# Second block's attention: a loop over tiles rewritten as a pipeline of eight units

## The chip, the cores and the metric

One core of one Trainium2 chip. The metric is the device time of one execution in microseconds; each kernel is run several times and the median is shown. Times inside an execution come from one execution taken with the hardware profiler.

## The reference, cut to what matters

The program is a whole network of three layers on 512 tokens of width 1024, all in float32: a first block (a mixer of a gated delta rule and a sliding window attention, then a mixture of 32 experts), then a second block of two layers, one with windowed attention and one with a recurrent unit, each followed by an MLP. The change lies in the second block's attention alone:

```
qkv = h @ w_in                                   # 512 x 1024 times 1024 x 1536
q, k, v = split: 8 heads of q, 2 of k, 2 of v, 128 wide; q, k = partial_rope(q), partial_rope(k)
kb, vb = band(k), band(v)                        # blocks n-1, n, n+1 of 128 keys, zeros outside
scores = einsum("bnqhgd,bnjhd->bnhgqj", qb, kb) * 128 ** -0.5
valid  = (|qpos - kpos| <= 128) & (kpos >= 0) & (kpos < 512)
scores = where(valid, scores, -inf)
m = maximum(max(scores), sink);  p = exp(scores - m)
denom = sum(p) + exp(sink - m)
o = einsum("bnhgqj,bnjhd->bnqhgd", p / denom, vb);  return o @ w_out
```

Four tiles of 128 queries, each against three blocks of 128 keys. The block before tile 0 and the block after tile 3 don't exist and are masked out.

## The kernel before, in words

Each engine has its own instruction list; between them stand semaphores that the program sets and waits for by hand. An engine takes its list in order. `drain` waits until the engine's own earlier work is written. `meet` (at the end of each stage) is a barrier over TensorE (pe), VectorE (dve), ScalarE (act) and GpSimd (pool); SyncE, which issues the weight loads, waits for barriers with `reached`.

The stage around the change is `at_pe`, `at_dve`, `at_act` and `at_loads`. In front of it `comb_dve` (line 1866) gathers the experts' outputs into X tile by tile, and SyncE loads the three 512-column pieces of `attn_w_in` into slots 0 to 2 and those of `attn_w_out` into slots 4 and 5. `piece_pe` (957) turns a tile of X with eight transposes into two PSUM banks and `piece_act` (968) writes it, scaled and shifted, into `hT`. PSUM has eight banks of 512 columns, `ps[:, 0]` to `ps[:, 7]`.

Projections (lines 1987 to 1999): for each tile three products of eight matmuls (L1996) with 512 columns; ScalarE copies each to `qtok` (L2098) and frees the bank; four banks are used in turn. A float32 matmul shows as two records in the trace, a float32 transpose as one. On VectorE the rope is applied per tile (2045 to 2051), and one semaphore, `roped`, is set after the last tile.

Then, once: k of all tiles is turned by eight transposes (L2006), copied to `kTa` (L2055), which has zero blocks at both ends, and v is copied to `vpad` with zero blocks (L2058).

Then a hardware loop (`Fori`) over the four tiles, on all three engines:

1. VectorE copies q of the tile to `stage` (L2061), TensorE turns its eight heads (L2011), VectorE copies them to `qTb` (L2063).
2. For each head g of k: TensorE makes the scores of four heads of q against 384 keys (L2018, four matmuls into banks 0 to 3). VectorE scales them, adds the mask and writes them to SBUF (L2068), takes the maximum (L2070), joins the sink and negates (L2072 to L2075). The scores of g = 1 wait for `att_shifted` of g = 0, since they use the same banks.
3. ScalarE takes the exponentials with their sums (L2105, L2107).
4. For each g: TensorE turns the twelve blocks of probabilities (L2023, banks 4 to 6), ScalarE copies them out (L2111), TensorE multiplies with v (L2030, bank 7), VectorE divides by the sum and writes the output into `qtok` (L2085).
5. The next tile begins when both outputs are written.

After the barrier `o_pe` turns the outputs (L965) and multiplies with `attn_w_out` (L2127). SyncE begins to load the weights of the following MLP only after the same barrier.

The first block's sliding window attention (`sw_pe`, `sw_act`, `sw_dve`, lines 999 to 1093) is written as eight units of a tile and a head of k, with the scores made two units ahead: scores L1070, shift L1011, maximum L1013, exponentials L1046, transposes L1083, copy L1058, product with v L1092, output L1024. Its heads are 64 wide, and a unit has two blocks of keys (one in tile 0).

Of the kernel before, what the change touches and what calls it, by code (L numbers as in the profile page):

```python
# [6 lines left out]
ALU = mybir.AluOpType  # L7
ACT = mybir.ActivationFunctionType
AX_X = mybir.AxisListType.X
# [98 lines left out]
def build(nc, A, out, dbg=None):  # L108
# [8 lines left out]
    with ctx:  # L117
# [1862 lines left out]
        vpad = scratch[:, 4096:5632].rearrange("p (b n) -> p b n", b=6)  # L1980

        def at_loads(sp):
            sp.dma_start(rope, A["k_rope"].rearrange("p (t b n) -> p t b n", t=TT, b=2)).then_inc(S("at_in"), 16)
            sp.dma_start(gqb, A["k_gqbias"].rearrange("p (t n) -> p t n", t=TT)).then_inc(S("at_in"), 16)

        def at_pe(pe):
            piece_pe(pe, "3", 0, X[:, 0], 4)
            for t in range(TT):
                turned(pe, "3", t)
                for s in range(3):  # L1990
                    if t == 0:
                        take(pe, s)
                    i = 3 * t + s
                    pe.wait_ge(S("bank_free"), before("bank_free", "at") + i + 1)
                    for k in range(KT):
                        ins = pe.matmul(ps[:, i % 4], hT[:, k, t * P:(t + 1) * P], slots[:, s, k], start=k == 0, stop=k == KT - 1)  # L1996
                    ins.then_inc(S("product"), 1)
                    if s == 0 and t + 1 < TT:
                        piece_pe(pe, "3", t + 1, X[:, t + 1], 4)
            for s in range(3):  # L2000
                pe.drain().then_inc(freed[s], 1)

            pe.wait_ge(S("roped"), 1)
            for g in range(KH):
                for t in range(TT):
                    ins = pe.transpose(ps[:, 4 + g, t * P:(t + 1) * P], qtok[:, t, QH * HD + g * HD:QH * HD + (g + 1) * HD], ident[:])  # L2006
            ins.then_inc(S("k_turned"), 1)
            with pe.Fori(0, TT) as t:
                pe.wait_ge(S("att_normed"), t + 1)
                for h in range(QH):  # L2010
                    ins = pe.transpose(ps[:, 6 + h // 4, (h % 4) * P:(h % 4 + 1) * P], stage[:, h * HD:(h + 1) * HD], ident[:])  # L2011
                ins.then_inc(S("att_turned"), 1)
                pe.wait_ge(S("att_qk_ready"), t + 1)
                for g in range(KH):
                    if g:
                        pe.wait_ge(S("att_shifted"), t * 2 + (g + NU))
                    for j in range(QK):
                        ins = pe.matmul(ps[:, j, 0:3 * P], qTb[:, g * QK + j], kTa[:, g, bass.ds(t * P, 3 * P)], start=True, stop=True)  # L2018
                    ins.then_inc(S("att_scores"), 1)
                for g in range(KH):  # L2020
                    pe.wait_ge(S("att_exp"), t * 2 + (g + 1 + NU))
                    for j in range(12):
                        ins = pe.transpose(ps[:, 4 + j // 4, (j % 4) * P:(j % 4 + 1) * P], glogs[g][:, j // 3, (j % 3) * P:(j % 3 + 1) * P], ident[:])  # L2023
                    ins.then_inc(S("att_pturned"), 1)
                    pe.wait_ge(S("att_pT"), t * 2 + (g + 1 + NU))
                    if g:
                        pe.wait_ge(S("att_tile_done"), t * 2 + (g + NU))
                    for j in range(QK):
                        for b in range(3):
                            ins = pe.matmul(ps[:, 7, j * P:(j + 1) * P], gpT[:, 3 * j + b], vpad[:, bass.ds(t + b, 1), g * HD:(g + 1) * HD], start=b == 0, stop=b == 2)  # L2030
                    ins.then_inc(S("att_pv"), 1)
                pe.wait_ge(S("att_tile_done"), t * 2 + (2 + NU))

        def at_dve(v):
            v.memset(kTa, 0.0)
            v.wait_ge(S("at_in"), 32)
            v.drain()
            H = ROT // 2
            for t in range(TT):
# [17 lines left out]
            v.memset(vpad[:, 5], 0.0)  # L2057
            v.tensor_copy(vpad[:, 1:5], qtok[:, :, 1280:1536])  # L2058
            v.drain()
            with v.Fori(0, TT) as t:  # L2060
                v.tensor_copy(stage[:], qtok[:, t, 0:D]).then_inc(S("att_normed"), 1)  # L2061
                v.wait_ge(S("att_turned"), t + 1)
                v.tensor_copy(qTb.rearrange("p (b h) n -> p b (h n)", b=2), ps[:, 6:8]).then_inc(S("att_qk_ready"), 1)  # L2063
                for g in range(KH):
                    mx, sk, nm = (small[:, 16 * g + 4 * j:16 * g + 4 * j + 4] for j in (0, 1, 3))
                    snk = sinks[:, SH + g * QK:SH + (g + 1) * QK]
                    v.wait_ge(S("att_scores"), t * 2 + (g + 1 + NU))
                    v.scalar_tensor_tensor(glogs[g], ps[:, 0:4, 0:3 * P], HD ** -0.5, gqb[:, bass.ds(t, 1)].broadcast_to([P, QK, 3 * P]), ALU.mult, ALU.add)  # L2068
                    v.drain()
                    v.tensor_reduce(mx, glogs[g], AX_X, ALU.max)  # L2070
                    v.drain()
                    v.tensor_tensor(mx, mx, snk, ALU.max)  # L2072
                    v.drain()
                    v.tensor_tensor(sk, snk, mx, ALU.subtract)
                    v.tensor_scalar(nm, mx, -1.0, None, ALU.mult)  # L2075
                    v.drain().then_inc(S("att_shifted"), 1)
                for g in range(KH):
                    sk, sm = (small[:, 16 * g + 4 * j:16 * g + 4 * j + 4] for j in (1, 2))
                    v.wait_ge(S("att_exp"), t * 2 + (g + 1 + NU))
                    v.tensor_tensor(sm, sm, sk, ALU.add)  # L2080
                    v.drain()
                    v.reciprocal(sm, sm)
                    v.drain()
                    v.wait_ge(S("att_pv"), t * 2 + (g + 1 + NU))
                    v.tensor_tensor(qtok[:, t, g * CH:(g + 1) * CH].rearrange("p (h d) -> p h d", h=QK), ps[:, 7].rearrange("p (h d) -> p h d", h=QK),  # L2085
# [596 lines left out]
```

## Time and profile before

| | us |
|---|---|
| median of 3 runs | 3620.05 |
| lowest, highest | 3616.89, 3629.53 |
| the profiled execution | 3626.3 |
| its span in the trace | 3624.6 |
| TensorE busy | 3104.3 (86%) |
| VectorE busy | 868.8 (24%) |
| ScalarE busy | 507.1 (14%) |
| GpSimd busy | 237.3 (7%) |
| moved by DMA | 646.73 MB, mean 178 GB/s |

Busy times count instructions at work, not waits. The span is the time between the first and the last instruction on record; the execution's own time is 1.7 us longer. The page divides the span into 40 slices of 90.6 us; the granted TensorE clock is given in tenths of 2.4 GHz, so 5 is 1.2 GHz. In the chain of waits, each piece of time belongs to the instruction that the next one waited for, and "issue" is time in which an engine waited for nothing that the profile shows.

### The profile page before, as it was taken

What the parts mean: (1) busy time and instruction counts of PE and PEld (TensorE: products, weight loads), DVE (VectorE), ACT (ScalarE), POOL (GpSimd) and SP (SyncE); (2) the same over time, 40 slices, a digit from 0 to 9 for tenths busy, and PEclk for the clock granted to TensorE, in tenths of its full rate; (3) what the DMA queues carried; (4) which work ended last, traced back from release to release, by engine and by line L of the source; (5) the groups of instructions that cost most, each with busy time, mean ns of one, the idle gap of its engine ahead of it and who ended that gap; (6) DMA issues with size and microseconds to landing.
All of it is one profiled execution on the core that took longest, in us unless ns stands there. A gap on an engine that the chain in (4) does not pass through costs nothing.

```text
span 3624.6 us, 36753 instructions
## 1 busy us (share of the span) xinstructions
PE 3104.3 (86%) x15370; PEld 1381.0 (38%) x15370; DVE 868.8 (24%) x1281; ACT 507.1 (14%) x986; POOL 237.3 (7%) x336
## 2 busy tenths in 40 slices
PE   7999978598999989999575889999699625999998
PEld 3465555232333333333244434444233202444443
DVE  2224243311111111111312220002330671200003
ACT  1030131000000000000112210001100850200001
POOL 0000011201110111101000000000100220000000
PEclk8989967799999999999787899999899757999999
DMA  7108931979999999999500211112220021212110
GB/s 255 47 7 335 340 104 41 342 301 404 381 405 403 402 401 406 405 405 388 227 0 0 105 64 69 69 58 70 72 72 29 17 51 48 91 66 93 69 70 23
DMA packets 167094, 646.73 MB, mean 178 GB/s; under 512 B 20091, under 2 KB 29883, under 8 KB 126337
## 3 DMA queue, kind: packets, MB, share of 16 engines
q1 hardware_dynamic: 151138, 605.91, 43.5%
q0 software_dynamic: 13952, 35.48, 3.3%
q10 hardware_dynamic: 1856, 3.21, 0.3%
q8 instruction: 112, 1.84, 0.2%
q14 instruction: 36, 0.29, 0.0%
HBM read 630.69 MB, written 18.38 MB: 179 GB/s over the span
## 4 chain that ended last, share of the span: by engine, by line
PE 49%; issue 31%; DVE 5%; DMA 5%; POOL 3%; PEld 2%; ACT 2%; POOLq 2%; DVEq 1%; PEldq 0%; ACTq 0%; SPq 0%
PE ps L2177 12%; PE ps L2188 12%; PE ps L2305 6%; PE ps L2481 3%; PE ps L1996 2%; DMA stage<-gate_dram 2%; DMA slots<-in_ada_w_dram 2%; PE ps L2127 2%; PE ps L1104 2%; POOLq L1536 2%; PE ps L314 1%; PE ps L2018 1%; POOL work L1545 1%; PEld ps L434 1%; PE ps L2030 1%
## 5 line engine op out<-in xcount | busy, mean ns | idle before, releaser
L1645 PE MATMUL ps<-slots,hT 128*32 128x512 f32 x5120 | 580.3, 598 | 18.3 <-DMA slots<-in_w_up_dram 7.6
L2177 PE MATMUL ps<-hT,slots 128*128 128x512 f32 x1024 | 448.9, 599 | 13.1 <-ACT hT L975 6.6
L2188 PE MATMUL ps<-slots,work 128*128 128x512 f32 x1024 | 441.8, 593 | 12.2 <-DVE work L2225 12.2
L1645 PEld LDWEIGHTS ps<-slots,hT 128*32 128x32 f32 x5120 | 160.6, 110 | 413.3 <-issue 396.6
L2177 PEld LDWEIGHTS ps<-hT,slots 128*128 128x128 f32 x1024 | 195.3, 192 | 265.9 <-issue 265.9
L2188 PEld LDWEIGHTS ps<-slots,work 128*128 128x128 f32 x1024 | 193.7, 190 | 258.8 <-issue 247.5
L1681 PE MATMUL ps<-slots,work 128*32 128x512 f32 x2112 | 254.5, 608 | 26.1 <-DMA slots<-in_w_down_dram 19.2
L2305 PE MATMUL ps<-hT,slots 128*96 128x512 f32 x512 | 223.7, 598 | 26.3 <-DVEq L2311 24.4
L2481 PE MATMUL ps<-slots,work 96*128 96x512 f32 x256 | 112.6, 602 | 107.4 <-DVE work L2468 107.4
L1796 DVE TENSOR_SCALAR stage<-ps 128x512 f32<-128x512 f32 (+1 forms) x47 | 32.2, 686 | 581.5 <-PE ps L1647 581.1
L1681 PEld LDWEIGHTS ps<-slots,work 128*32 128x32 f32 x2112 | 90.4, 112 | 157.9 <-issue 124.6
L2305 PEld LDWEIGHTS ps<-hT,slots 128*96 128x96 f32 x512 | 83.5, 164 | 166.0 <-issue 166.0
L2216 ACT ACTIVATE stage<-ps 128x512 f32<-128x512 f32 x64 | 38.2, 597 | 759.6 <-PE ps L2177 759.6
L2225 DVE TENSOR_TENSOR work<-stage 128x512 f32<-128x512 f32 x64 | 44.3, 693 | 400.1 <-ACT stage L2216 400.1
L1774 ACT ACTIVATE modA<-stage 128x512 f32<-128x512 f32 (+1 forms) x47 | 29.6, 630 | 639.1 <-DVE stage L1796 639.1
L2481 PEld LDWEIGHTS ps<-slots,work 96*128 96x128 f32 x256 | 49.2, 193 | 169.4 <-issue 169.4
L2238 DVE TENSOR_TENSOR work<-work,ps 128x512 f32<-128x512 f32 x48 | 33.0, 688 | 303.3 <-PE ps L2188 303.3
L1996 PE MATMUL ps<-slots,hT 128*128 128x512 f32 x192 | 85.6, 606 | 3.0 <-ACT hT L975 3.0
L434 PE MATMUL ps<-hT,slots 128*128 128x512 f32 x192 | 85.3, 606 | 1.9 <-DVEq L460 1.4
L1816 DVE COPY modB<-ps 128x512 f32<-128x512 f32 x33 | 22.8, 692 | 247.3 <-PE ps L1684 238.6
L314 PE MATMUL ps<-slots,modA 128*32 128x512 f32 x512 | 65.9, 629 | 14.1 <-DMA slots<-in_ada_w_dram 10.0
L2359 PE MATMUL ps<-work 96*96 96x512 f32 x64 | 42.1, 745 | 39.3 <-ACT slots L2381 24.6
(547 smaller groups left out, 2980.2 us busy)
## 6 DMA issues: line engine op xcount, KB each, us to landing
slots<-in_w_up_dram SPq DMA_DIRECT2D x128, 2048.0 KB, 18.6
slots<-in_w_down_dram SPq DMA_DIRECT2D x64, 2048.0 KB, 17.3
slots<-in_mlp_w_dram SPq DMA_DIRECT2D x32, 2048.0 KB, 8.6
slots<-in_ada_w_dram SPq DMA_DIRECT2D x16, 2048.0 KB, 9.5
slots<-in_w_ada_dram SPq DMA_DIRECT2D x12, 2048.0 KB, 8.6
slots<-in_ada_w_dram SPq DMA_DIRECT2D x16, 1024.0 KB, 7.0
slots<-in_rnn_w_in_dram SPq DMA_DIRECT2D x8, 1536.0 KB, 6.9
slots<-in_w_in_dram SPq DMA_DIRECT2D x5, 2048.0 KB, 17.4
```

What stands on the lines that cost most here:

```text
L314: ins = pe.matmul(ps[32 * j:32 * j + 32, 6 + g % 2], ada_c[:, which, 2 * q + kk], ada_slots[:, s, kk, j * CH:(j + 1) * CH], start=q + kk = ...
L434: ins = pe.matmul(ps[:, m], slots[:, s, k, m * P:(m + 1) * P], hT[:, k, :], start=k == 0, stop=k == KT - 1)
L1104: ins = pe.matmul(ps[:, 2 * (t % 2) + h], hT[:, k, t * P:(t + 1) * P], slots[:, 4 + h, k], start=k == 0, stop=k == KT - 1)
L1536: g.drain()
L1645: ins = pe.matmul(to, x[:, k, unit * UNIT:(unit + 1) * UNIT], upw[s][:, k % 2, col:col + CH], start=k == 0, stop=False)
L1681: ins = pe.matmul(to, actT[:, 4 * q + j, 64 * u + 32 * h:64 * u + 32 * h + 32], downw[sl[h]][:, j, half * CH:(half + 1) * CH], start=k == ...
L1996: ins = pe.matmul(ps[:, i % 4], hT[:, k, t * P:(t + 1) * P], slots[:, s, k], start=k == 0, stop=k == KT - 1)
L2127: ins = pe.matmul(ps[:, 2 * (t % 2) + h], hT[:, k, t * P:(t + 1) * P], slots[:, 4 + h, k], start=k == 0, stop=k == KT - 1)
L2177: ins = pe.matmul(ps[:, m], slots[:, s, k, m * P:(m + 1) * P], hT[:, k, :], start=k == 0, stop=k == KT - 1)
L2188: ins = pe.matmul(ps[:, 4 + 2 * (t % 2) + h], h1T[:, k, t * P:(t + 1) * P], slots[:, 2 + h, k], start=k == 0, stop=k == KT - 1)
L2305: ins = pe.matmul(ps[0:RW, m], slots[:, s, k, m * RW:(m + 1) * RW], hT[:, k, :], start=k == 0, stop=k == KT - 1)
L2481: ins = pe.matmul(ps[:, 2 * (t % 2) + h], xr[:, n, t * P:(t + 1) * P], slots[0:RW, s0 + n // 8, n % 8], start=n == 0, stop=n == RB - 1)
```

## The change

The attention becomes eight units i = 0 to 7, tile i // 2 and head of k i % 2. Keys outside the sequence are left out: units of tiles 0 and 3 have two blocks of keys, the others three. q and k of a tile are turned right after the projection of the next tile (`turn_qk`) and stay turned for all tiles (`kTg`, `qTg`); v is read from `qtok`. Scores lie gapless in banks 0 to 2 and are made two units ahead; they wait for `att_read`, which VectorE sets when the shift has read the banks. The product alternates between banks 3 and 7. The hardware loops become written-out ones. The mask is the same 384 columns for every tile, so only these are loaded.

```diff
         qtok = work[:, 0:6144].rearrange("p (t n) -> p t n", t=TT)
-        kTa = work[:, 6144:7680].rearrange("p (g n) -> p g n", g=KH)
-        qTb = work[:, 7680:8704].rearrange("p (h n) -> p h n", h=QH)
-        glog = work[:, 8704:10240].rearrange("p (h n) -> p h n", h=QK)
+        kTg = work[:, 6144:7168].rearrange("p (g n) -> p g n", g=KH)
+        qTg = slots[:, 3]
+        glog = [work[:, 8704:10240], hT[:].rearrange("p k t -> p (k t)")[:, 0:3 * CH]]
         gpT = work[:, 10240:11776].rearrange("p (j n) -> p j n", j=12)
-        gqb = work[:, 11776:13312].rearrange("p (t n) -> p t n", t=TT)
+        gqb = work[:, 11776:12160]
...
         def at_loads(sp):
             sp.dma_start(rope, A["k_rope"].rearrange("p (t b n) -> p t b n", t=TT, b=2)).then_inc(S("at_in"), 16)
-            sp.dma_start(gqb, A["k_gqbias"].rearrange("p (t n) -> p t n", t=TT)).then_inc(S("at_in"), 16)
+            sp.dma_start(gqb, A["k_gqbias"][:, 3 * P:6 * P]).then_inc(S("at_in"), 16)
+
+        NG = TT * KH
+
+        def near(t):
+
+            return range(1 if t == 0 else 0, 2 if t == TT - 1 else 3)
+
+        def gunit(i):
+
+            t, g = i // KH, i % KH
+            bs = near(t)
+            mx, nm_, sk, sm = (small[:, 16 * (i % 4) + 4 * j:16 * (i % 4) + 4 * j + 4] for j in range(4))
+            return t, g, bs, len(bs) * P, mx, nm_, sk, sm
...
-                    i = 3 * t + s
-                    pe.wait_ge(S("bank_free"), before("bank_free", "at") + i + 1)
+                    pe.wait_ge(S("bank_free"), before("bank_free", "at") + 4 + (3 * t - 2 + s if t else 0))
                     for k in range(KT):
-                        ins = pe.matmul(ps[:, i % 4], hT[:, k, t * P:(t + 1) * P], slots[:, s, k], start=k == 0, stop=k == KT - 1)
+                        ins = pe.matmul(ps[:, s], hT[:, k, t * P:(t + 1) * P], slots[:, s, k], start=k == 0, stop=k == KT - 1)
                     ins.then_inc(S("product"), 1)
                     if s == 0 and t + 1 < TT:
-                        piece_pe(pe, "3", t + 1, X[:, t + 1], 4)
+                        piece_pe(pe, "3", t + 1, X[:, t + 1], 4 - 2 * ((t + 1) % 2))
+
+            def turn_qk(t):
+                pe.wait_ge(S("roped"), t + 1)
+                if t:
+                    pe.wait_ge(S("att_qk_ready"), t)
+                for g in range(KH):
+                    ins = pe.transpose(ps[:, 3, g * P:(g + 1) * P], qtok[:, t, QH * HD + g * HD:QH * HD + (g + 1) * HD], ident[:])
+                for h in range(QH):
+                    ins = pe.transpose(ps[:, 6 + h // 4, (h % 4) * P:(h % 4 + 1) * P], qtok[:, t, h * HD:(h + 1) * HD], ident[:])
+                ins.then_inc(S("att_turned"), 1)
+
+            def scores(i):
+                t, g, bs, n, *_ = gunit(i)
+                pe.wait_ge(S("att_qk_ready"), min(t + 2, TT))
+                pe.wait_ge(*((S("att_read"), i) if i else (S("bank_free"), before("bank_free", "at") + 4 + 3 * TT)))
+                for j in range(QK):
+                    c = j * n
+                    while c < (j + 1) * n:
+                        e = min((j + 1) * n, c // CH * CH + CH)
+                        k0 = (t - 1 + bs[0]) * P + c - j * n
+                        ins = pe.matmul(ps[:, c // CH, c % CH:c % CH + e - c], qTg[:, g * QK + j, t * P:(t + 1) * P], kTg[:, g, k0:k0 + e - c], start=True, stop=True)
+                        c = e
+                ins.then_inc(S("att_scores"), 1)
+
+            piece_pe(pe, "3", 0, X[:, 0], 4)
+            for t in range(TT):
+                products(t)
+                if t:
+                    turn_qk(t - 1)
             for s in range(3):
...
-            pe.wait_ge(S("roped"), 1)
-            for g in range(KH):
...
-            with pe.Fori(0, TT) as t:
-                pe.wait_ge(S("att_normed"), t + 1)
-                for h in range(QH):
...
-                pe.wait_ge(S("att_qk_ready"), t + 1)
-                for g in range(KH):
...
-                    ins.then_inc(S("att_scores"), 1)
-                for g in range(KH):
-                    pe.wait_ge(S("att_exp"), t * 2 + (g + 1 + NU))
...
-                    ins.then_inc(S("att_pturned"), 1)
-                    pe.wait_ge(S("att_pT"), t * 2 + (g + 1 + NU))
-                    if g:
-                        pe.wait_ge(S("att_tile_done"), t * 2 + (g + NU))
...
-                    ins.then_inc(S("att_pv"), 1)
-                pe.wait_ge(S("att_tile_done"), t * 2 + (2 + NU))
+            scores(0)
+            turn_qk(TT - 1)
+            scores(1)
+            for i in range(NG):
+                t, g, bs, n, *_ = gunit(i)
+                pe.wait_ge(S("att_exp"), NU + i + 1)
+                if i:
+                    pe.wait_ge(S("att_pT"), NU + i)
+                else:
+                    pe.wait_ge(S("att_qk_ready"), TT)
+                for c in range(QK * len(bs)):
+                    ins = pe.transpose(ps[:, 4 + c // 4, (c % 4) * P:(c % 4 + 1) * P], glog[i % 2][:, c * P:(c + 1) * P], ident[:])
+                ins.then_inc(S("att_pturned"), 1)
+                if i + 2 < NG:
+                    scores(i + 2)
+                pe.wait_ge(S("att_pT"), NU + i + 1)
+                if i >= 2:
+                    pe.wait_ge(S("att_tile_done"), NU + i - 1)
+                for j in range(QK):
+                    for m, b in enumerate(bs):
+                        ins = pe.matmul(ps[:, 3 + 4 * (i % 2), j * P:(j + 1) * P], gpT[:, j * len(bs) + m], qtok[:, t - 1 + b, 1280 + g * HD:1280 + (g + 1) * HD],
+                                        start=m == 0, stop=m == len(bs) - 1)
+                ins.then_inc(S("att_pv"), 1)
+            pe.wait_ge(S("att_tile_done"), NU + NG)
...
-                v.drain()
-            v.drain().then_inc(S("roped"), 1)
-            v.wait_ge(S("k_turned"), 1)
-            v.tensor_copy(kTa[:, :, P:P + T], ps[:, 4:6])
-            v.memset(vpad[:, 0], 0.0)
...
-            v.tensor_copy(vpad[:, 1:5], qtok[:, :, 1280:1536])
-            v.drain()
-            with v.Fori(0, TT) as t:
-                v.tensor_copy(stage[:], qtok[:, t, 0:D]).then_inc(S("att_normed"), 1)
+                v.drain().then_inc(S("roped"), 1)
+
+            def qk_out(t):
+                c = slice(t * P, (t + 1) * P)
                 v.wait_ge(S("att_turned"), t + 1)
-                v.tensor_copy(qTb.rearrange("p (b h) n -> p b (h n)", b=2), ps[:, 6:8]).then_inc(S("att_qk_ready"), 1)
-                for g in range(KH):
...
+                v.tensor_copy(kTg[:, :, c], ps[:, 3, 0:KH * P].rearrange("p (g n) -> p g n", g=KH))
+                v.tensor_copy(qTg[:, :, c], ps[:, 6:8].rearrange("p b (h n) -> p (b h) n", n=P)).then_inc(S("att_qk_ready"), 1)
...
+            def shifted(i):
...
+                lg4 = glog[i % 2][:, 0:QK * n].rearrange("p (h n) -> p h n", h=QK)
+                raw = ps[:, 0:3].rearrange("p b n -> p (b n)")[:, 0:QK * n].rearrange("p (h n) -> p h n", h=QK)
+                v.wait_ge(S("att_scores"), NU + i + 1)
+                if i >= 2:
+                    v.wait_ge(S("att_pturned"), NU + i - 1)
+                v.scalar_tensor_tensor(lg4, raw, HD ** -0.5, gqb[:, bs[0] * P:bs[0] * P + n].unsqueeze(1).broadcast_to([P, QK, n]), ALU.mult, ALU.add).then_inc(S("att_read"), 1)
+                v.drain()
...
+                v.drain().then_inc(S("att_shifted"), 1)
+
+            def out_of(i):
+                t, g, bs, n, mx, nm_, sk, sm = gunit(i)
+                v.wait_ge(S("att_pv"), NU + i + 1)
+                v.tensor_tensor(qtok[:, t, g * CH:(g + 1) * CH].rearrange("p (h d) -> p h d", h=QK), ps[:, 3 + 4 * (i % 2)].rearrange("p (h d) -> p h d", h=QK),
...
+            roped(0)
+            for t in range(1, TT):
+                roped(t)
+                qk_out(t - 1)
+            shifted(0)
+            qk_out(TT - 1)
+            shifted(1)
+            for i in range(NG):
+                t, g, bs, n, mx, nm_, sk, sm = gunit(i)
+                v.wait_ge(S("att_exp"), NU + i + 1)
+                v.tensor_tensor(sm, sm, sk, ALU.add)
+                v.drain()
+                v.reciprocal(sm, sm)
+                if i + 2 < NG:
+                    shifted(i + 2)
+                v.drain()
+                out_of(i)
+            v.drain()
...
-            with a.Fori(0, TT) as t:
...
-                exps(0)
-                exps(1)
-                probs_out(0)
-                probs_out(1)
+                        piece_act(a, "3", t + 1, 4 - 2 * ((t + 1) % 2), 0)
...
+                a.wait_ge(S("att_shifted"), NU + i + 1)
...
+            exps(0)
+            for i in range(NG):
+                if i + 1 < NG:
+                    exps(i + 1)
+                c = QK * len(near(i // KH)) * P
+                a.wait_ge(S("att_pturned"), NU + i + 1)
+                if i:
+                    a.wait_ge(S("att_pv"), NU + i)
+                a.copy(gpT.rearrange("p j n -> p (j n)")[:, 0:c], ps[:, 4:7].rearrange("p b n -> p (b n)")[:, 0:c]).then_inc(S("att_pT"), 1)
```

## Rows read from the trace of the kernel before

**Rows 1.** The page's slices: granted TensorE clock, tenths, one digit per slice

```profile
PEclk8989967799999999999787899999899757999999
```

**Rows 2.** Windows: the stage, one tile, a stretch of the first block's attention

```profile
core 0: us, PE busy (x) PEld busy (x) DVE busy (x) ACT busy (x) POOL busy (x), PEclk, DMA share, GB/s
1864.58:2027.48 162.90, 92.16 (x392) 68.09 (x392) 50.80 (x82) 37.52 (x85) 0.00 (x0) 0.73 0.00 0
...
1911.70:1949.50 37.80, 21.23 (x96) 16.02 (x96) 11.72 (x18) 9.23 (x21) 0.00 (x0) 0.77 0.00 0
...
490.00:498.00 8.00, 8.00 (x49) 6.66 (x50) 4.58 (x15) 3.07 (x10) 0.00 (x0) 0.69 0.01 2
```

**Rows 3.** Chain of waits in the stage: start, duration, engine, output, line, records

```profile
1864.58 0.59 ACT work L2098
...
1866.99 1.95 PE ps L2006 x8
...
1872.29 1.98 PE ps L2011 x8
1874.29 1.24 DVE work L2063
...
1899.29 5.47 PE ps L2030 x24
...
1919.72 1.76 DVE work L2068
1921.55 1.75 DVE small L2070
...
1924.03 5.06 PE ps L2018 x8
...
1933.32 2.50 ACT hT L2105 x8
...
1937.39 5.20 PE ps L2030 x24
1942.59 1.32 PE ps L2023 x12
1943.93 1.45 ACT work L2111
...
1945.52 2.95 PE ps L2030 x24
1948.61 0.69 DVE work L2085
```

**Rows 4.** Chain of waits, projection of tile 2

```profile
1808.73 20.60 PE ps L1996 x48
```

**Rows 5.** Chain of waits in the first block's attention

```profile
476.40 1.28 ACT L1046
...
484.39 1.22 DVE small L1013
...
486.23 2.08 ACT slots L1046 x8
...
501.34 3.35 PE ps L1092 x16
504.69 1.71 PE ps L1083 x8
506.40 2.03 PE ps L1070 x8
...
512.02 0.05 ACT slots L1046
...
515.14 3.48 PE ps L1092 x16
...
520.37 1.02 ACT slots L1058
```

**Rows 6.** Timeline, one product of the first block's attention: start, duration, shape

```profile
494.54 2.16 PE L1092 MATMUL ps<-work,slots 128*128 128x64 f32 x16
```

More of the change, by code:

```diff
@@ L2034, in at_dve, with roped @@
+            pe.wait_ge(S("att_tile_done"), NU + NG)
         def at_dve(v):
-            v.memset(kTa, 0.0)
+            H = ROT // 2
             v.wait_ge(S("at_in"), 32)
-            v.drain()
-            H = ROT // 2
-            for t in range(TT):
+            def roped(t):
                 v.wait_ge(S("bank_free"), before("bank_free", "at") + 4 + 3 * (t + 1))
@@ new lines, in shifted @@
+            def shifted(i):
+                t, g, bs, n, mx, nm_, sk, sm = gunit(i)
+                snk = sinks[:, SH + g * QK:SH + (g + 1) * QK]
+                lg4 = glog[i % 2][:, 0:QK * n].rearrange("p (h n) -> p h n", h=QK)
[4 more added lines that the diff above has]
+                v.scalar_tensor_tensor(lg4, raw, HD ** -0.5, gqb[:, bs[0] * P:bs[0] * P + n].unsqueeze(1).broadcast_to([P, QK, n]), ALU.mult, ALU.add).then_inc(S("att_read"), 1)
+                v.drain()
+                v.tensor_reduce(mx, lg4, AX_X, ALU.max)
+                v.drain()
+                v.tensor_tensor(mx, mx, snk, ALU.max)
+                v.drain()
+                v.tensor_tensor(sk, snk, mx, ALU.subtract)
+                v.tensor_scalar(nm_, mx, -1.0, None, ALU.mult)
+                v.drain().then_inc(S("att_shifted"), 1)
@@ L2095, in at_act, with exps @@
                 for s in range(3):
-                    i = 3 * t + s
-                    a.wait_ge(S("product"), before("product", "at") + i + 1)
-                    a.copy(qtok[:, t, s * CH:(s + 1) * CH], ps[:, i % 4]).then_inc(S("bank_free"), 1)
+                    a.wait_ge(S("product"), before("product", "at") + 3 * t + s + 1)
+                    a.copy(qtok[:, t, s * CH:(s + 1) * CH], ps[:, s]).then_inc(S("bank_free"), 1)
                     if s == 0 and t + 1 < TT:
-                        piece_act(a, "3", t + 1, 4, 0)
-            with a.Fori(0, TT) as t:
-                def exps(g):
-                    a.wait_ge(S("att_shifted"), t * 2 + (g + 1 + NU))
-                    for j in range(QK):
-                        a.activation(glogs[g][:, j], glogs[g][:, j], ACT.Exp, bias=small[:, 16 * g + 12 + j:16 * g + 13 + j],
-                                     accum_out=small[:, 16 * g + 8 + j:16 * g + 9 + j])
-                    a.activation(small[:, 16 * g + 4:16 * g + 8], small[:, 16 * g + 4:16 * g + 8], ACT.Exp).then_inc(S("att_exp"), 1)
-                def probs_out(g):
-                    a.wait_ge(S("att_pturned"), t * 2 + (g + 1 + NU))
-                    a.copy(gpT.rearrange("p (b j) n -> p b (j n)", b=3), ps[:, 4:7]).then_inc(S("att_pT"), 1)
-                exps(0)
-                exps(1)
-                probs_out(0)
-                probs_out(1)
+                        piece_act(a, "3", t + 1, 4 - 2 * ((t + 1) % 2), 0)
+            def exps(i):
+                t, g, bs, n, mx, nm_, sk, sm = gunit(i)
+                a.wait_ge(S("att_shifted"), NU + i + 1)
+                for j in range(QK):
+                    p_ = glog[i % 2][:, j * n:(j + 1) * n]
+                    a.activation(p_, p_, ACT.Exp, bias=nm_[:, j:j + 1], accum_out=sm[:, j:j + 1])
+                a.activation(sk, sk, ACT.Exp).then_inc(S("att_exp"), 1)
+            exps(0)
[7 more added lines that the diff above has]
+                a.copy(gpT.rearrange("p j n -> p (j n)")[:, 0:c], ps[:, 4:7].rearrange("p b n -> p (b n)")[:, 0:c]).then_inc(S("att_pT"), 1)
         def o_pe(pe):
```

46 lines of the change are left out of this document (4 added, 42 removed).

## The prediction

> **What bounds the kernel now.** The slices of the page come first [rows 1]: the granted clock stands near its full level but for three dips. The dip in slices 20 to 23 holds the second block's attention. The windows put its ends: between the last projection and the first transpose of the output product lie 162.9 us [rows 2], in which TensorE is busy 92.2, VectorE 50.8 and ScalarE 37.5, with a mean granted clock of 0.73. So no engine is the bound; the busy times together (180.5) are hardly more than the stretch, which says that the engines take turns. No transfer runs in it. The chain of waits shows the turns [rows 3]: scores 5.1, shift 1.76, maximum 1.75, small operations, exponentials 2.50, copy 1.4, probabilities times v 5.2, transposes, copy 1.45, second product 2.95, output 0.69, and the next tile only begins when the last output is written. One tile costs 37.8 us (the second window), four cost 151, and 12 are the lead-in. The scores stand at 5.06 us for eight records of 384 columns. At full clock a record of 512 columns takes 20.60 / 48 = 0.429 us [rows 4], so eight of 384 would take 2.6: the scores run at 1.2 GHz, because TensorE has just waited 4 to 7 us for the other engines. The chain pays for the waits twice, as idle time and as clock.
>
> What follows the stage waits for its end: the barrier, and behind it all loads of the next MLP's weights. These keep their distance to it, as do the matmuls that hide them. The change leaves that alone, so a microsecond won in the stage is one won at the end.
>
> **Prices of one unit** (a tile and a head of k). Three-block units, tiles 1 and 2, at 2.4 GHz: 12 transposes 1.4 (1.32 plus a start) [rows 3]; scores 2.6, plus 0.1 because the bank borders cut them into six matmuls instead of four: 2.7; product with v 2.95. TensorE: 7.0 us. At 1.2 GHz: 2.9 (from 1.98 for eight), 5.2, 5.5: 13.6. VectorE: 1.76 + 1.75 and the small ones, 4.1 to 4.3 from the shift's begin to the next step's (1919.72 to 1924.03), later 0.5 + 0.7. ScalarE: 2.5 + 1.43. Two-block units, tiles 0 and 3, are two thirds: transposes 0.95, scores 1.8, product 2.0, so 4.8 us (9.2 at 1.2 GHz); VectorE 1.22 + 1.22 + 0.6 = 3.1, with the maximum over 1024 elements and, by the nearest row, the shift at the same; ScalarE 2.1 for the exponentials and 1.0 for the copy [rows 5]. Handing over between engines costs about 0.1 to 0.15 each time, the "issue" gaps of the chain.
>
> **The new loop.** TensorE does transposes of unit i, scores of i+2, product of i. The scores of i+2 do not wait for the exponentials of i+1, only for the reading of their banks, so two units are in flight. ScalarE does the exponentials of i+1 before it copies the transposed probabilities of i. The cycle that closes is: end of scores i+1, VectorE 4.1, ScalarE 2.5, ScalarE copy of unit i 1.43, product of i 2.95, transposes of i+1 1.4, scores of i+3 2.7. It spans two units. With five handovers (0.7) it is 15.8, so 7.9 us a unit against 7.0 of TensorE work: some 0.9 idle per unit. Two-block units give 3.1 + 2.1 + 1.0 + 2.0 + 0.95 + 1.8 + 0.7 = 11.6, so 5.8. The first block's attention is already written in this order, and checks the form: its products of units 3 and 5 begin 13.80 us apart [rows 5], 6.9 a unit, where the same cycle with its own durations (product 3.4, transposes 1.7, scores 2.0, VectorE 3.6 from 508.43 to 512.02, ScalarE 2.1 + 1.0) gives 13.8 with most handovers inside it, 6.9 a unit.
>
> **The sum, part by part.**
> Removed from between the projections and the output: everything, 162.9 us.
> Lead-in: last projection copied out and rope applied, 2.4 (from 1864.58 to 1866.99) [rows 3]. Then q and k of tile 2 leave PSUM on VectorE, 0.4 + 1.24, the turned q being in front of the first shift in VectorE's order: 4.1. Shift and maximum of unit 0, 3.1: 7.2. ScalarE's table load, 1.28: in the old loop it hid at the head of the loop, in the first block it stands on the chain [rows 5], and I count it. Exponentials 2.1: transposes of unit 0 begin at 10.6. The turning of tile 3 and the scores of units 0 and 1 fit into this.
> Units: 4 x 7.9 + 4 x 5.8 = 54.8. Last output: 0.8. Together 66.2.
> Turning q and k of tiles 0 and 1 between the projections: ten transposes each, 1.32 us per twelve [rows 3], put into a TensorE stream with no gap: + 2.2 to 2.8, on the path. I take 2.2, the price without a pause. The waits in front (rope, the earlier turn out) have a whole tile's projection, 20.6 us, to be met; if that cover were gone each would cost the 2.4 of the rope.
> Clock: TensorE idles about 3.4 us before the transposes of unit 0, a gap of the size after which the old stage ran at 1.2, so its first burst is slow: between 0 and one unit's difference (6.6); I take 1.7, since the second product of the tile, behind 5 us of steady work, is fast again (5.20, then 1.32 and 2.95) [rows 3]. In the tail there are no scores to fill, the product of unit 6 waits 2.6 and that of 7 1.3: 0 to 4.4 (two slow two-block units less scores); I take 3. The output product may then start slow: 0 to 3, taken 1.5.
> Edits at nothing: one copy of q less per tile and the padding of k and v (VectorE 0.7 and less; on the old chain, thus in the 162.9); the smaller bias load on POOL's queue, issued long before (its cover gone, some 2 us once); three product banks for four, as the copy of 0.59 has two products of 6.9 to finish in; the pieces of X in two banks alternately used by neither q nor each other, as each is read before the next tile's first product.
> Total 66.2 + 2.2 + 1.7 + 3 + 1.5 = 74.6 against 162.9: **88 us gained**. The profiled execution took 3626.3 (span 3624.6) and would take 3538. The median shown is 6 lower, 3620.05, so for the median I forecast 3532.
>
> **Bounds.** Everything fast and no dip: 66.2 + 2.2 = 68, minus the table load if it hides, 67: 96 gained, 3524; with the scatter of the runs shown, 3518. On the slow side see the rivals.
>
> **Rivals.**
> (a) The clock swings all through. For: the first block's attention, the same order, had a stretch at 0.69 in its middle [rows 2]. Against: its product moves 64 columns where this one moves 128 [rows 6], and its TensorE work at full clock is some 4.0 us of 6.9 (2.16 for the product [rows 6], half of 1.7 and of 2.0), while here it is 7.0 of 7.9. At a mean of 0.75 a three-block unit has 9.3 us of work and the cycle gives (8.7 + 9.3) / 2 = 9.0, a two-block unit (6.9 + 6.4) / 2 = 6.6: 4 x 1.1 + 4 x 0.8 = 8 more, so 3540. The Trainium skill (TensorE: Matmul & The Clock Gate, "A second HAM failure mode: psum-queue depth-cycling") says that a loop which cycles PSUM banks with small pauses between its groups can lose throughput to a clock going up and down. That is this rival; the rows of the first block's attention agree, those of the projections, which also cycle banks but without pauses, do not show it.
> (b) The clock stays at 1.2 GHz. Then TensorE is the bound: 4 x 13.6 + 4 x 9.2 = 91, less the scores of units 0 and 1 that lie in the lead-in (7.0), plus lead-in 11.6, waits of the tail 2.6, output 0.8: 99, with turns and a slow start of what follows 103. Gain 60: 3560. Against: the old stage reaches full clock after one slow product [rows 3]; here TensorE would be busy without any pause.
> (c) **Slower than before.** TensorE takes its queue in order: the transposes of unit i wait for its exponentials, and the scores of i+2 stand behind them. If this wait ends last in every unit, units follow each other instead of overlapping, and every burst is cold: 5.2 + 4.1 + 2.5 + 2.9 + 1.4 + 5.5 + 0.7 + 1.0 for handovers = 23.3, the two-block one 17.0; eight are 161.2, lead-in 9, turns 2.2, slow start 1.5: 174, 11 more than before, 3631. It decides once a mean unit takes over 18.8 us. Against: two units' scores are made before the loop, and in the first block's attention the same order overlapped.
> (d) The change does not do what it says, or the gain is waited for later by a load: against it, no transfer of the stage or of the barrier behind it has a time of its own. About no change.
>
> **How the numbers follow.** Forecast (clock mostly full, 3518 to 3544): 0.66. (a) 3540, between 3534 and 3550: 0.19. (b) 3560: 0.10. (c): 0.03. (d): 0.02. 3518 to 3556 leaves out (b), (c) and (d), and a little of the forecast's low end: some 2 in 10. A change under 0.3%, 11 us, is about what a measurement of this kernel can't tell from none; only (d) lies there. Faster 0.96, same 0.015, slower 0.025.
>
> **What the profile would show.** The output product's first transpose some 73 us after the last projection; the products of units 2 to 5 beginning 7 to 9 us apart; TensorE idle before the product of each unit, released by ScalarE's copy, 0.5 to 2 us, and not before the scores; a pause of 3 to 4 us before the first transposes of unit 0; granted clock over 0.85 between. Scores at 2.7 (5.2 would be rival b), one table load, the projections 2 us longer. I am wrong if units take over 10 us, if transposes wait for exponentials in the middle of the loop, or if the stretches after the stage change length.

## The result, and the profile after

| | before | after |
|---|---|---|
| median of 4 runs, us | 3622.68 | 3524.36 |
| lowest, highest | 3616.89, 3629.53 | 3513.73, 3530.77 |
| span of the profiled execution | 3624.6 | 3520.1 |
| last projection to first transpose of the output product | 163.1 | 66.3 |
| first to last projection | 87.7 | 90.2 |

The ratio of the two is 0.973, with a 95% interval of 0.9715 to 0.9745: 98 us faster. The prediction had 88 and a range that holds the result. The two traces differ by 104.5 us of span. Of these, 94.4 lie in the two stretches of the last two rows (96.8 won, 2.4 given back), 0.7 behind them, and 9.4 in front, where the change touches nothing: the first projection begins at 1776.8 in the trace of before and at 1767.4 here. In the traces of the kernels below that leave the first block alone it begins anywhere from 1765 to 1783. So the whole run is a coarse ruler for this change, and the two stretches are the fine one.

Windows of the changed kernel: lead-in, units 0 and 1, units 2 and 3, units 4 and 5, tail, the output product, and the whole stage (columns as in [rows 2]).

```profile
1857.53:1871.40 13.87, 9.84 (x56) 7.50 (x54) 11.43 (x23) 6.20 (x21) 0.00 (x0) 1.00 0.00 0
1871.40:1886.10 14.70, 11.49 (x76) 9.53 (x76) 10.60 (x17) 8.31 (x22) 0.00 (x0) 1.00 0.00 1
1886.10:1901.20 15.10, 12.66 (x92) 11.30 (x92) 10.24 (x17) 7.84 (x20) 0.00 (x0) 1.00 0.01 2
1901.20:1915.10 13.90, 11.24 (x76) 10.64 (x76) 5.29 (x15) 6.67 (x20) 0.00 (x0) 0.88 0.00 0
1915.10:1923.70 8.60, 6.63 (x40) 6.06 (x40) 1.63 (x4) 1.01 (x1) 0.00 (x0) 0.80 0.01 2
...
1857.53:1923.73 66.20, 51.86 (x340) 45.04 (x338) 39.20 (x74) 30.04 (x82) 0.00 (x0) 0.95 0.00 1
```

Against [rows 2], whose window ends 0.2 us before the first transpose, the stage's 162.9 us at a clock of 0.73 with 92.2 of TensorE have become 66.2 at 0.95 with 51.9 of TensorE. VectorE and ScalarE are down from 50.8 and 37.5 to 39.2 and 30.0. Their busy times add up to 121 in 66 us: the engines overlap now. The clock is full until unit 4.

The chain of waits in the middle and at the end of the loop, against [rows 3]:

```profile
1886.12 2.94 PE ps L2061 x24
1889.06 1.31 PE ps L2052 x12
1890.37 2.62 PE ps L2030 x12
...
1893.01 1.76 DVE hT L2099
...
1894.86 1.75 DVE small L2101
...
1897.75 1.98 ACT hT L2149 x7
...
1899.83 1.33 ACT work L2160
...
1901.20 4.35 PE ps L2061 x24
1905.55 1.54 PE ps L2052 x12
```

Scores are L2030, the shift L2099, exponentials L2149, transposes L2052, the copy L2160, the product L2061. This is the cycle that the prediction wrote down: scores, VectorE, the exponentials of the newer unit, and only then the copy of the older one, for which the product waits. The products of units 2 and 4 begin 15.08 us apart. Scores take 2.62, about half of the 5.06 in [rows 3]. The product of unit 4 took 4.35 where that of unit 2 took 2.94: the clock had just fallen.

What TensorE waited for (line <- releaser: us in total, times, longest):

```profile
PE ps L2061 <- ACT work L2160: 10.3, 6, 2.7
PE ps L2052 <- ACT small L2150: 2.0, 1, 2.0
PE ps L965 <- DVEq L193: 1.0, 1, 1.0
```

The second line is the lead-in, the third the output product behind the barrier. In the timeline the waits before products are, in order: 1.87 (unit 0), 0.41, 1.86, none, 2.42 (unit 4), none, 2.69 and 1.10. The even units wait, the odd ones don't.

### The profile page after: what moved, and what is told of

It reads as the page before. It is cut to its first block, busy times and chain, and to the rows that moved or that the text cites. A ratio compares the mean times of both kernels' runs of the same rounds, so it can differ in the third digit from the quotient of the medians.

```text
span 3520.1 us, 36607 instructions
## 1 busy us (share of the span) xinstructions
PE 3058.4 (87%) x15338; PEld 1354.6 (38%) x15338; DVE 858.9 (24%) x1276; ACT 499.0 (14%) x983; POOL 236.1 (7%) x336
## 3 DMA queue, kind: packets, MB, share of 16 engines
q8 instruction: 114, 1.87, 0.2%
## 4 chain that ended last, share of the span: by engine, by line
PE 49%; issue 32%; DMA 5%; DVE 5%; POOL 3%; PEld 2%; ACT 2%; POOLq 2%; DVEq 1%; PEldq 0%; ACTq 0%; SPq 0%
PE ps L2221 13%; PE ps L2232 13%; PE ps L2349 6%; PE ps L2525 3%; PE ps L2006 2%; DMA stage<-gate_dram 2%; DMA slots<-in_ada_w_dram 2%; PE ps L2171 2%; PE ps L1104 2%; POOLq L1536 2%; PE ps L314 1%; POOL work L1545 1%; PEld ps L434 1%; PE ps L245 1%; DVE slots L2494 1%
## 5 line engine op out<-in xcount | busy, mean ns | idle before, releaser
L2232 PE MATMUL ps<-slots,work 128*128 128x512 f32 x1024 | 441.8, 593 | 12.2 <-DVE work L2269 12.2
L1681 PEld LDWEIGHTS ps<-slots,work 128*32 128x32 f32 x2112 | 90.2, 111 | 158.6 <-issue 126.6
```

The lines of the kernel that those rows point to most:

```text
L1681: ins = pe.matmul(to, actT[:, 4 * q + j, 64 * u + 32 * h:64 * u + 32 * h + 32], downw[sl[h]][:, j, half * CH:(half + 1) * CH], start=k == ...
L2232: ins = pe.matmul(ps[:, 4 + 2 * (t % 2) + h], h1T[:, k, t * P:(t + 1) * P], slots[:, 2 + h, k], start=k == 0, stop=k == KT - 1)
```

## The experiments

"Stage" is from the end of the last projection to the first transpose of the output product, in the experiment's own trace. It was the same, 66.3, in two traces of the changed kernel. Where no ratio is given, the kernel was run once, and the argument rests on its stage alone, not on its whole time.

**Three blocks everywhere.** The pads of k are zero and the old mask is loaded, so the computation is complete.

```diff
-            return range(1 if t == 0 else 0, 2 if t == TT - 1 else 3)
+            return range(0, 3)
```

> The pipeline with three blocks in every unit: the keys outside the sequence are computed and masked, as in the kernel before. Theory: skipping shortens units 0, 1, 6, 7 only, so with it undone each of them costs what a middle unit costs: the stage (66.3 us from the last projection to the first transpose of the output product) grows by 7 to 10 us, 1.5 to 2.5 of it in the lead-in. Rival, that the loop hides the absent blocks in waits for ScalarE anyway: under 3 us.

Measured: stage 78.9, 12.6 more; more than the expectation or its rival said. The chain shows why:

```profile
1872.23 1.33 ACT work L2162
1873.60 5.49 PE ps L2061 x24
...
1891.54 2.94 PE ps L2061 x24
...
1906.62 2.94 PE ps L2061 x24
...
1921.70 5.49 PE ps L2061 x24
```

The products of the first and of the seventh unit come after longer waits (up to 3.9 us, where the longest was 2.7) and run at the low clock: 2 x 2.55 us. The same kernel with the swap on ScalarE, below, takes this apart.

**The turns after the projections.**

```diff
             for t in range(TT):
                 products(t)
-                if t:
-                    turn_qk(t - 1)
...
+            for t in range(TT - 1):
+                turn_qk(t)
```

(and on VectorE all ropes, then the copies of the turned q and k.)

> q and k of tiles 0 to 2 are turned after the last projection. Theory: the projections get 2.4 us shorter, but three turns and their copies on VectorE then stand one behind the other before the first shift: the lead-in grows by 5 to 6.5 us, net 3 to 4 slower. Rival, that the turns cost the same in either place since TensorE waits in the lead-in anyway: net within 1 us.

Measured: projections 88.15 (2.0 less), stage 75.3 (9.0 more), net 7.0 slower. The chain of the lead-in:

```profile
1867.65 0.41 PE ps L2016 x2
1868.06 0.89 PE ps L2018 x8
...
1868.97 0.42 DVE work L2088
1869.40 1.14 DVE slots L2089
...
1870.67 0.66 PE ps L2016 x2
1871.33 1.71 PE ps L2018 x8
1873.04 3.43 PE ps L2030 x8
```

The turns do wait for each other's copies. In addition the third turn and the scores of unit 0 run at the low clock (0.66 and 1.71 where 0.41 and 0.89 are the times at full clock; 3.43 where unit 7 has 1.74), 2.8 us together. That is most of the 3 to 4 us that the expectation missed. Early turning wins 9.0 in the stage and costs 2.0 in the projections: 7.0 net, of which 2.8 is clock.

**No look-ahead.** The scores of the next unit stand behind the wait for this unit's output, and VectorE and ScalarE take one unit at a time too; early turns and skipping stay.

```diff
-                if i + 2 < NG:
-                    scores(i + 2)
...
                 ins.then_inc(S("att_pv"), 1)
+                pe.wait_ge(S("att_tile_done"), NU + i + 1)
+                if i + 1 < NG:
+                    scores(i + 1)
```

> No look-ahead: the scores of a unit are made after the output of the unit before is written; the early turns and the skipping stay. Theory (overlap and clock both pay): units of 23.3 us with three blocks and 17.0 with two, scores at 5.1 us, mean clock near 0.6: stage about 170 us, 100 more than with look-ahead, so slower than the kernel before. Rival (the clock matters little and the waits are what counted): scores at 2.7, units of 16.8 and 12.6, stage 127, 60 more.

Measured: stage 146.0, one run 3616.8 beside 3628.5 for the kernel before. Windows of its units 2 to 5:

```profile
1904.69:1926.87 22.18, 12.96 (x49) 10.79 (x49) 4.95 (x8) 4.03 (x10) 0.00 (x0) 0.60 0.00 0
1926.87:1944.72 17.85, 8.63 (x49) 7.06 (x49) 4.95 (x8) 4.03 (x10) 0.00 (x0) 0.81 0.00 0
1944.72:1964.70 19.98, 10.76 (x49) 9.19 (x49) 4.95 (x8) 4.03 (x10) 0.00 (x0) 0.66 0.00 1
1964.70:1984.91 20.21, 10.99 (x49) 9.42 (x49) 4.95 (x8) 4.03 (x10) 0.00 (x0) 0.66 0.00 0
```

It falls between the two accounts. Unit 2 takes 22.2 us, near the 23.3 that was priced for the low clock, unit 3 17.9, near the 16.8 of the full one, and units 4 and 5 lie between with 20.0 and 20.2: scores take 4.84 in unit 2 and 2.88 in the others, products 5.33, 2.96, 5.08 and 5.32. The look-ahead is worth 80 us (146.0 to 66.3). What is left, 163.1 to 146.0 less 2.1 for the turns in the projections, is 15. That this is the skipping, the early turns and the written-out loop, set against the overlap of two heads inside a tile that the old loop had and this variant lacks, is an account of the code; no run parts it. The loop's own share can be read: in the chain of the kernel before, 0.49 us lie between the end of a tile's output (1911.47) and the copy that begins the next tile (1911.96), so some 2 us in four tiles.

**The kernel before, with its waits filled.** Matmuls that nothing reads, in free banks.

```diff
+            def fill(bank, n):
+                for _ in range(n):
+                    pe.matmul(ps[:, bank], ident[:], slots[:, 0, 0], start=True, stop=True)
...
+                        fill(5, 4)
                         pe.wait_ge(S("att_shifted"), t * 2 + (g + NU))
...
+                    fill(*((0, 1) if g else (7, 6)))
                     pe.wait_ge(S("att_pT"), t * 2 + (g + 1 + NU))
```

> The kernel before with unused matmuls put where TensorE waits in the attention loop: 6 while ScalarE copies the first head's probabilities, 4 while the first head is shifted, and 1, 1 and 2 elsewhere. The order of the real work is as before. Theory: the clock was a good third of the old stage's cost: granted clock near 1.0, scores 2.6 in place of 5.1 to 5.5, first product 2.95 in place of 5.2, stage 162.9 to about 132. Rival (the clock is not what made the scores slow, or fillers cost what they give): 160 or more.

Measured: stage 140.0, granted clock 0.94, 3603.7 beside 3628.5. Its chain (scores L2024, product L2037):

```profile
1909.70 2.86 PE ps L2024 x8
...
1917.01 2.86 PE ps L2024 x8
...
1928.17 2.94 PE ps L2037 x24
...
1960.02 4.57 PE ps L2037 x24
```

Scores 5.06 [rows 3] became 2.86, the product 5.20 became 2.94, in the order of before. So at least 23 us of the old stage were the price of the clock alone, and a kernel can win them by doing more. It is 8 short of the expected 31: the products of tiles 2 and 3 still ran slow (4.57, 4.39), the first scores too (3.38), and the others stand at 2.86 where 2.6 was counted; together that is some 6 of the 8. The waits were the larger payment: TensorE stood still for 71 of the old stage's 162.9 us (162.90 less 92.16 [rows 2]).

**One swap on ScalarE.** It is the remedy for what the profile after shows.

```diff
             for i in range(NG):
-                if i + 1 < NG:
-                    exps(i + 1)
...
                 a.copy(gpT...).then_inc(S("att_pT"), 1)
+                if i + 1 < NG:
+                    exps(i + 1)
```

> The changed kernel with one swap on ScalarE: the copy of unit i's turned probabilities comes before the exponentials of unit i+1. Theory: what stood in the loop was this order, 10.3 us of waiting before the products in six waits, and one fall of the clock behind them; with the swap TensorE is the bound, units of 7.1 and 4.8 us, only the last two products wait (1.3 us each), stage 66.3 to about 57. Rival (the exponentials then come late and the transposes wait instead): stage within 2 us of 66.

**The changed kernel again**, beside it on one chip.

> The changed kernel unaltered, on the chip of the two others: stage 66 us, a time 2.7% under the kernel before; the swap should be 0.2 to 0.3% under it.

Measured in five rounds each: the swap 3519.4, ratio to the kernel before 0.9697 (0.9681 to 0.9714); the changed kernel 3535.7, ratio 0.9737 (0.9724 to 0.9751). The stages are 54.1 and 66.3. The intervals do not touch; 12.2 of the 16 us between the medians are seen in the stage. That is more than expected, 0.4% in place of 0.2 to 0.3% and 54.1 in place of 57: a three-block unit takes 6.6 us (products at 1894.54 and 1901.13) where 7.1 was counted. Waits of the swapped kernel, the same columns as above:

```profile
PE ps L2061 <- ACT work L2158: 2.2, 2, 1.1
PE ps L2052 <- ACT small L2150: 2.0, 1, 2.0
```

and its window, to set beside the 66.20 above:

```profile
1870.71:1924.81 54.10, 47.77 (x340) 42.30 (x339) 39.10 (x74) 30.23 (x82) 0.00 (x0) 1.00 0.00 1
```

The six waits of 10.3 us together are now two of 2.2 together, those in the tail, where no scores are left to cover the copy. The slow bursts from unit 4 on, which cost 3.3 us in the changed kernel, are gone too. So of the 12.2 us some 8.1 are waits and 3.3 clock. TensorE is busy 47.8 of 54.1 at full clock: it is the bound. The exponentials are not far behind it: those of units 3 and 4 end 1.15 us before their transposes begin, those of units 2 and 7 only some 0.05.

**The last unit turned early.** Unit 7's probabilities go to banks 0 and 1, right behind unit 6's, and on ScalarE the exponentials of unit 7 come before the copy of unit 6.

```diff
                 if i < NG - 1:
                     turn_p(i)
+                if i == NG - 2:
+                    turn_p(i + 1)
```

> As the swap, and the last unit's probabilities are turned right behind those of unit 6, into banks 0 and 1, with a place of their own in SBUF. Theory: one wait of a copy less in the tail, 1 to 1.5 us under the swap alone, stage about 56. Rival: the transposes of unit 7 wait for its exponentials in front of the product of unit 6, nothing won.

Measured: stage 55.2, 1.1 more than with the swap alone; 3524.2, ratio 0.9712 (0.9698 to 0.9725), which overlaps the swap's. Nothing won; the rival holds. Its waits and chain:

```profile
PE ps L2054 <- ACT small L2159: 4.3, 2, 2.3
```

```profile
1909.15 2.07 ACT hT L2158 x8
...
1911.38 1.69 PE ps L2054 x8
1913.07 4.63 PE ps L2070 x32
```

The transposes of unit 7 stand 2.3 us waiting for their exponentials, in front of the product of unit 6, and the clock has fallen behind that wait (1.69 for eight transposes).

**Three blocks everywhere, with the swap.**

> Three blocks in every unit and the copy first on ScalarE. Theory: undoing the skipping cost 12.6 us with the other order, of which some 5 were two products that ran at the low clock after longer waits (5.49 where 2.94 is the price at full clock), so with TensorE kept busy it costs its work alone, about 9.5: stage 63 to 65 against 54.1. Rival (the 12.6 are all work and waits of the absent blocks): 66 to 67.

Measured: stage 63.6, clock 1.00. Against 54.1 the skipping is worth 9.5 us: TensorE's busy time falls from 56.1 to 47.8, and the waits in the lead-in and the tail get 1.2 shorter. The other 3 of the 12.6 were the clock and the waits of the unswapped order, as the theory had it.

**The changed kernel, with two filling matmuls before the product of each even unit.**

```diff
-                pe.wait_ge(S("att_pT"), NU + i + 1)
                 if i >= 2:
                     pe.wait_ge(S("att_tile_done"), NU + i - 1)
+                if i % 2 == 0:
+                    for _ in range(2):
+                        pe.matmul(ps[:, 3 + 4 * (i % 2)], ident[:], slots[:, 0, 0], start=True, stop=True)
+                pe.wait_ge(S("att_pT"), NU + i + 1)
```

> The changed kernel with two unused matmuls (1.7 us at full clock) in the wait before the product of every even unit; nothing else moves. It parts the 12.2 us that the swap on ScalarE won into clock and waits. Theory: the clock falls before the products of units 4 and 6 only, worth some 3 us: stage 66.3 to about 63, granted clock 1.00, and the other 9 us of the swap are waits. Rival (most of the swap's gain is clock): under 60. Rival (fillers cost as much as they give): 66 or more.

Measured: stage 64.5, clock 0.97, 1.8 less where some 3 were expected. The fillers did their part: the products of units 4 and 6 and the transposes behind them ran fast. But the scores of unit 2, which stand before the first filler, ran at the low clock here and not in the changed kernel:

```profile
1870.07 1.09 PE ps L2052 x8
1871.17 4.29 PE ps L2030 x12
```

That put every later step back by 1.7 us. The wait in front of these transposes is 2.04, as in the changed kernel. So the fillers are worth 3.5 us (1.8 and 1.7), which agrees with the 3.3 us of slow bursts counted in the changed kernel: some 3.5 of the swap's 12.2 were clock. Most of the rest were waits, 10.3 against 2.2.

**The swap in both attentions.** The same two lines in `sw_act` of the first block.

> The swap in the second block's attention and the same swap in the first block's attention. Theory: there too the exponentials in front of the copy hold up the product; the first block's attention, some 59 us from its first scores to its last output, falls by 4 to 9 us, and the whole by the same under the swap alone. Rival (TensorE has too little to do there and stays at the low clock, where its 7.1 us of work per unit are the bound with either order): nothing won there.

Measured in five rounds: 3499.5 beside 3623.5, ratio 0.9659 (0.9644 to 0.9674), the fastest kernel of the study: 3.4% under the kernel before, where the change alone is 2.6 to 2.7% under it. Its second block's stage was 55.8, and not 54.1, since the scores of unit 2 took 4.28 us here too. The first block's attention, from its first scores to its last output, without and with the swap there:

```profile
475.07:533.84 58.77, 41.86 (x233) 35.81 (x233) 30.18 (x89) 24.45 (x81) 9.54 (x10) 0.67 0.21 44
```

```profile
481.92:525.52 43.60, 35.45 (x232) 29.03 (x232) 30.03 (x89) 24.53 (x81) 9.56 (x10) 0.77 0.27 58
```

It fell by 15.2 us, where 4 to 9 were expected. The waits before its products went from 11.5 us in six to 2.2 in two. TensorE's busy time fell by 6.4 with the same work, as the clock rose from 0.67 to 0.77. Its chain is now one of ScalarE:

```profile
509.04 0.91 ACT slots L1056
509.95 2.08 ACT slots L1046 x8
...
512.18 1.11 PE ps L1083 x8
513.31 0.99 ACT slots L1056
```

A period of 4.3 us: copy, exponentials, transposes, copy. The rival had taken 7.1 us of TensorE work a unit at the low clock for the floor; in these units TensorE ran at the full one (transposes 1.11, where 1.71 is in [rows 5]).

## Why the prediction was right, point by point

**What bounded the old stage** held. The filled kernel shows the two payments apart: 23 us or more for the clock, and the look-ahead took the waits, 80 us from the serial variant with whatever clock went with them. One reason given does not fit all rows: the scores were slow "because TensorE has just waited 4 to 7 us", but in front of the first head's scores it waited 1.4 us, behind eight transposes and a wait of 2.1 (3.4 in tile 0), and they ran at 4.35 to 5.50.

**The cycle** held in form and nearly in size: 15.08 and 15.85 us for two three-block units (products of units 2 to 4 and 3 to 5) where 15.8 was forecast. The first is the clean one: from the end of one unit's scores (1877.90) to that of the scores two units on (1892.99) everything ran at full clock, and of the 0.7 us less than forecast most is handing over, 0.2 in place of 0.7. That the second equals the forecast is luck, since it holds 1.6 us of slow bursts and a two-block unit's scores. The wait that ends the cycle, ScalarE's copy behind the exponentials of the next unit, was named; the swap proves it, as the waits go and nothing else was touched. Only its distribution was not foreseen: the cycle spans two units, so one wait of 1.9 to 2.7 falls on every second product in place of 0.9 on each. In this trace the clock fell behind the two longest of them, 2.42 and 2.69.

**The sum**: 74.6 forecast, 66.3 + 2.4 = 68.7 measured. The steps that were off, in the prediction's order:
- The table load on the chain, 1.28: it was not on it. It started at 1858.16, as the last projection's copy ended, and was over 2 us before the first shift began, so the transposes of unit 0 began at 9.3 and not at 10.6.
- The slow first burst, 1.7: nothing here. TensorE waited 2.0, not 3.4, and the granted clock stayed at 1.00. That is in part luck: the same wait of 2.04 stands in seven traces of this pipeline, and in two of them (the changed kernel with fillers, and the swap in both attentions) the clock fell behind it and cost these 1.7 us.
- Units, output and tail: 54.8 + 0.8 + 3 = 58.6 forecast from there, 57.05 measured. The fall of the clock in the tail came, and earlier than said, at unit 4: products of 4.35 and 2.90 and transposes of 1.54 and 1.69 cost some 3.3 us against their times at full clock, where 3 was taken. Half of that, at unit 4, was not in the prediction's account of the tail, so the size agrees by luck; what made this part shorter is the units' cycle.
- The output product starting slow, 1.5: nothing; its first 32 records take 14.00 us in both traces.
- Turns in the projections: 2.4 against 2.2.

These are 1.3 + 1.7 + 1.6 + 1.5 less 0.2, the 5.9 that the sum was too high. The result lies near the fast end of the prediction, where 67 to 68 was given for no dip at all. The remaining 4 us of the 98 against 88 lie outside the two stretches, in code that the change leaves alone, and within the scatter seen there.

**The rivals.** (a), a clock that swings all through, came in part: 0.88 and 0.80 in the last two windows, 1.00 before. What the Trainium skill says under "A second HAM failure mode: psum-queue depth-cycling" (TensorE: Matmul & The Clock Gate), that small pauses between groups of matmuls cost throughput through the clock, agrees with the product at 4.35 us behind a wait of 2.42, and with the first block's attention; but waits of 1.87 and 1.86 before the products of units 0 and 2 were not followed by it. (b) did not happen. (c) was priced at 174 us for the stage and the projections' turns; with no look-ahead at all it is 148. So serial units would have lost to the pipeline by 80 us and still have had a stage some 15 faster than before. Two steps of that sum were wrong. "Every burst is cold" accounts for 15 of the 24 us by which the stage was overpriced: units 2 to 6 took less than their prices of 23.3 and 17.0 (22.2, 17.9, 20.0, 20.2 and 15.0). The other 9 were counted twice: the transposes of unit 0 began 9.3 us after the last projection, so the lead-in of 9 already holds its scores, shift and exponentials. As far as this one variant can tell, the rival does not lie on the slow side of no change, where it was put. (d) did not happen: behind the stage the traces differ by 0.7 us in 1597.

**The parts**, each undone alone: look-ahead 80, skipping 12.6 (9.5 once the clock holds), early turning 7.0. They make 99 where the whole is 94.4, so they are not independent. The written-out loops, some 2 us by the chain, and the product's two banks were not undone alone. The sum did not price skipping and early turning by themselves. For the skipping its unit prices give 4 x 2.1 and 1.5 in the lead-in, 9.9, which is what was found at full clock.

## What to carry to other kernels

When one engine serves two units of a pipeline, put first what the bounding engine needs soonest: a copy that a matmul waits for goes ahead of the next unit's exponentials, if these still end before their transposes are due (here with 0.05 to 1.15 us to spare; in the tail variant they did not, and nothing was won). Write down the cycle with the units' numbers, and see how many units it spans: a cycle over two units puts its whole wait on every second one (1.9 to 2.7 us here, not 0.9 on each). A stage in which TensorE keeps stopping costs its waits and its clock; filling matmuls (here 23 us of 163) tell the two apart in one run. Compare such a run burst by burst and not by its total: in the second filled kernel a slow burst elsewhere hid half of what the fillers gave.

## What was not expected of the hardware

The same work behind the same wait can run at either level. In the seven traces of the pipeline with two-block first units, the transposes of unit 0 follow a wait of 2.04 us and the scores of unit 2 come right behind them; in five these scores took 2.6 us, in two 4.3. One of each kind, the swap alone and the swap in both attentions, show the same TensorE work and the same waits from the last projection to there. Nor does the length of a wait part the cases: in the filled kernel before, the product behind a wait of 1.85 took 2.94 in tiles 0 and 1 and 4.57 and 4.39 in tiles 2 and 3; in the changed kernel the product behind 1.86 was fast and the one behind 2.42 slow.

A TensorE with long waits is not always at the low clock. In the variant with no look-ahead it was busy 8.6 of 17.9 us in unit 3 and yet at a clock of 0.81, and the scores of units 3 to 5 took 2.88, while the scores of units 1 and 7 ran at the low level (3.80 for eight records of 256 columns, where 1.74 is the fast one). Which of the bursts are slow changes from unit to unit with the same work and waits (products of 5.33, 2.96, 5.08 and 5.32). The fillers show the other side: two products of the filled kernel before stayed slow (4.57 and 4.39) where TensorE was busy 35.7 of 41 us (1960 to 2001). What decides this is open.
